# The square output matrices of S5, RG-LRU and RWKV as split three-term products

## The chip, the cores and the metric

One core of one Trainium2 chip runs the whole program. The metric is the device time of one execution in microseconds (us); the median of three runs is compared. The engines are TensorE (PE, with its weight loads shown as PEld), VectorE (DVE), ScalarE (ACT), GpSimd (POOL) and SyncE (SP), which here only issues the loads of weights.

## The reference, cut to what matters

A decoder trunk of two layers over 256 positions of width 1024, all in fp32. The part that the change touches is the hybrid mixing in the middle of each layer:

```python
    y_s5 = (y @ glu_w1) * jax.nn.sigmoid(y @ glu_w2)      # y: GELU of the S5 output, 512 channels
    ...
    y_lru = (h * jax.nn.gelu(zy)) @ lru_w_out             # h: RG-LRU scan
    ...
    y_rw = ((y + bonus) * g) @ rw_w_out                   # y: normalised RWKV-7 output
    ...
    merged = gates[:, :, 0] * y_s5 + gates[:, :, 1] * y_lru + gates[:, :, 2] * y_rw
    x = layer_norm(ALPHA * x + merged @ mix_w_out[l], ln2_g[l], ln2_b[l])
```

Around it stand a SwiGLU block before, cross-attention and a second SwiGLU block after. The four matrices glu_w1, glu_w2, lru_w_out and rw_w_out have 512 rows and 1024 columns; each layer has its own.

## The kernel before

Every weight matrix is cut into pieces of 128 x 1024 elements (512 KB). SP loads the pieces in one fixed order, `PIECES`, into a ring of 6 slots, `ring_raw`; a slot is loaded again when the piece in it has been multiplied (`s_piece`).

Most weights are multiplied as a split product. ACT copies a piece rounded to fp32r into `ring_hi`, a ring of only 3 slots (`hi_to`, through the helper at L1177; before the cast of split piece i it waits until split piece i - 3 has been multiplied). Then DVE (`lo_to`, L1564) or POOL (`piece_lo`, L2106) writes the remainder, raw minus hi, over the raw piece as `ring_lo`. `POOL_LO` lists the pieces whose remainder POOL takes, among them all of the branch gates; the rest is DVE's. The other operand is split the same way into a hi and a lo tensor. PE multiplies with `mm3` (L676, L677, L678): hi x hi, hi x lo, lo x hi, three fp32r matmuls into one bank.

The four square matrices are different: `PLAIN` names them (w1, w2, lru, rw), they are not cast and have no remainder, and `half_chunk` multiplies the raw piece by the unsplit fp32 operand (L689), 8 matmuls of 128 x 128 by 128 x 256 for each half chunk, which the profile records as 16. A chunk is 256 output columns in two halves m = 0 and 1 for the gates; a square chunk is 512 columns in two halves, 4 halves for each matrix. There are 32 such halves in the program.

Each engine runs a program written by hand, in order; `hi_to(kind, j, m)` means: cast all pieces up to this one, and with `further` also the next if it follows directly in `PIECES`. So where a cast stands in ACT's program decides when it can run, whatever the slots allow. In the middle of a layer the order is:

- ACT: the last GELUs of S5 (4 on `zu`), a wait for the RG-LRU result `ly` (`s_yl`), 8 sigmoids for RWKV's decay and in-context rate, gate evacuations, the exponentials of the RWKV decay, 4 scalings by r_k (`s_rks`), then the sigmoid of w2's product.
- DVE: 4 scans (L1826), each followed by a product (L1827), which give `ly`; then scans of the decay (L1834) and products L1836 to L1866, which build RWKV's operands, and in them the last reader of the first exponentials (L1859), for which ACT's third exponential waits.
- POOL: the remainders of gates 0 to 3, then nothing until it clears `W_bd` (L2177, L2178), which waits for the operands.
- PE: gates 0 to 3, the small RWKV products (L915 is the last of them and waits for 4 of ACT's sigmoids), w1 chunk 0, w2 chunk 0, the bonus sums (L926, which waits for `s_rks`), transposes (L932, L941) with the halves of w1 chunk 1 between, the products G (L956), w2 chunk 1, N (L965), gate 4.

Then comes the triangular solve: five rounds of small products and transposes (L977, L996, L1005), with a half chunk after each product; the fillers are gates 5, 6, 7 and lru 0, 1. The state recurrence over four chunks follows (L1021 to L1058) with gates 8 to 11 as fillers, and then the memory's k and v projections, rw chunks 0 and 1 between v 0 and v 1, and the output projection `mix`. `merge` on DVE (L1882, L1883, L1888, L1889) gathers the branches.

## Time and profile before

| | us |
|---|---|
| median of three runs | 1926.34 |
| lowest, highest | 1925.96, 1928.41 |
| profiled execution | 1927.2 |
| span in its trace | 1925.4 |
| PE busy | 1766.2 |
| DVE busy | 1251.6 |
| ACT busy | 778.7 |
| POOL busy | 601.9 |

The span runs from the first to the last instruction of the profiled execution. A matmul's recorded length contains its way through the array, so consecutive records overlap, and the cost of a block of matmuls is read from the start of its first record to the start of the next block. The two layers lie 948.5 us apart in the trace.

### The profile page before, as it was taken

The numbers are of one execution on the slowest core, as the hardware profiler recorded it, in microseconds if no ns is written. First come the engines' busy times: TensorE is split into PE (matmuls) and PEld (weight loads), VectorE is DVE, ScalarE is ACT, GpSimd is POOL, SyncE is SP. The second block draws the span as 40 slices with busy tenths as digits, with TensorE's granted clock in tenths as the row PEclk, the third lists the DMA queues.
The fourth block names the chain that finished last, engine by engine and source line by source line (L and its number), as shares of the span: only waits on it lengthen the run. The fifth ranks groups of instructions, "written<-read, shape, count | busy, mean of one in ns | idle before, by whom it ended". The sixth has DMA issues, their size and how long they took to land.

```text
span 1925.4 us, 29408 instructions
## 1 busy us (share of the span) xinstructions
PE 1766.2 (92%) x12308; PEld 1602.5 (83%) x12308; DVE 1251.6 (65%) x1430; ACT 778.7 (40%) x998; POOL 601.9 (31%) x370
## 2 busy tenths in 40 slices
PE   5999888888999999999999997988889899999997
PEld 5989866777988988899989896767789888879996
DVE  4587889985343675744476877999653365765445
ACT  3445512362224344544455444115521243544442
POOL 1141377522431030411151415774133400322112
PEclk9999988899899999999999999879998999999998
DMA  6655533332133554566666564223322345445663
GB/s 192 184 179 183 161 87 88 110 99 77 56 95 92 192 158 137 160 185 185 200 182 187 175 185 144 68 85 116 93 78 60 98 127 187 143 136 181 185 185 123
DMA packets 380603, 267.57 MB, mean 139 GB/s; under 512 B 21084, under 2 KB 361400, under 8 KB 380472
## 3 DMA queue, kind: packets, MB, share of 16 engines
q1 hardware_dynamic: 377624, 255.22, 44.5%
q10 hardware_dynamic: 2848, 10.49, 1.6%
q8 instruction: 97, 1.59, 0.3%
q14 instruction: 34, 0.28, 0.0%
HBM read 264.62 MB, written 1.05 MB: 138 GB/s over the span
## 4 chain that ended last, share of the span: by engine, by line
PE 64%; DVE 23%; issue 6%; ACT 3%; POOL 3%; DMA 1%; SPq 0%; DVEq 0%; POOLq 0%; ACTq 0%
PE bank L676 16%; PE bank L678 16%; PE bank L677 16%; DVE ring_lo L1564 5%; PE bank L689 5%; PE bank L996 2%; ACT ring_hi L1177 1%; PE bank L1005 1%; DVE work L1748 1%; DVE region_z L1944 1%; POOL work L2193 1%; DVE work L1752 1%; ACT work L1177 1%; DVE work L1785 1%; DVE small L1583 1%
## 5 line engine op out<-in xcount | busy, mean ns | idle before, releaser
L1564 DVE TENSOR_TENSOR ring_lo<-ring_raw,ring_hi 128x1024 fp32r<-128x1024 f32 x390 | 531.6, 1368 | 370.7 <-ACT ring_hi L1177 358.2
L1177 ACT ACTIVATE ring_hi<-ring_raw 128x1024 fp32r<-128x1024 f32 x444 | 468.0, 1057 | 587.8 <-PE bank L678 547.5
L676 PE MATMUL bank<-xT_hi,ring_hi 128*128 128x256 f32 x2224 | 650.7, 293 | 20.9 <-DVE ring_lo L1564 9.9
L677 PE MATMUL bank<-xT_lo,ring_hi 128*128 128x256 f32 x2224 | 641.1, 288 | 0.0
L678 PE MATMUL bank<-xT_hi,ring_lo 128*128 128x256 f32 x2224 | 640.3, 288 | 0.0
L676 PEld LDWEIGHTS bank<-xT_hi,ring_hi 128*128 128x128 f32 x2224 | 439.3, 198 | 37.9 <-issue 21.4
L677 PEld LDWEIGHTS bank<-xT_lo,ring_hi 128*128 128x128 f32 x2224 | 439.5, 198 | 1.8
L678 PEld LDWEIGHTS bank<-xT_hi,ring_lo 128*128 128x128 f32 x2224 | 438.8, 197 | 0.0
L2112 POOL TENSOR_TENSOR hT_lo<-work,hT_hi 128x512 fp32r<-128x512 f32 x44 | 79.4, 1807 | 508.5 <-ACT hT_hi L1177 508.0
L2106 POOL TENSOR_TENSOR ring_lo<-ring_raw,ring_hi 128x1024 fp32r<-128x1024 f32 x54 | 138.0, 2556 | 246.7 <-ACT ring_hi L1177 245.0
L678 PE MATMUL bank<-ring_hi,hT_lo 128*128 128x512 f32 x352 | 140.5, 399 | 0.0
L677 PE MATMUL bank<-ring_lo,hT_hi 128*128 128x512 f32 x352 | 140.2, 398 | 0.0
L676 PE MATMUL bank<-ring_hi,hT_hi 128*128 128x512 f32 x352 | 138.8, 394 | 0.9 <-POOL hT_lo L2112 0.5
L1177 ACT ACTIVATE work<-bank 128x512 f32<-128x512 f32 x94 | 53.9, 597 | 155.9 <-PE bank L678 69.4
L689 PE MATMUL bank<-region_z,ring_raw 128*128 128x256 f32 x384 | 87.2, 383 | 0.5 <-DVE region_a L1883 0.5
L689 PEld LDWEIGHTS bank<-region_z,ring_raw 128*128 128x128 f32 x384 | 72.7, 192 | 11.0 <-issue 0.9
L676 PEld LDWEIGHTS bank<-ring_hi,hT_hi 128*128 128x128 f32 x352 | 68.0, 193 | 15.7 <-issue 0.7
L2166 POOL TENSOR_TENSOR work<-work,region_r 128x512 f32<-128x512 f32 x32 | 66.3, 2072 | 46.9 <-DVE work L1752 46.9
L2080 POOL TENSOR_TENSOR small<-small,constants 128x1 f32<-128x1 f32 x16 | 10.9, 683 | 220.0 <-DVE small L1585 220.0
L678 PEld LDWEIGHTS bank<-ring_hi,hT_lo 128*128 128x128 f32 x352 | 66.7, 189 | 14.3
L677 PEld LDWEIGHTS bank<-ring_lo,hT_hi 128*128 128x128 f32 x352 | 66.8, 190 | 13.5
L1940 DVE TENSOR_TENSOR region_z<-bank,constants 128x512 f32<-128x512 f32 x20 | 13.8, 691 | 88.8 <-PE bank L1005 88.8
(277 smaller groups left out, 2729.1 us busy)
## 6 DMA issues: line engine op xcount, KB each, us to landing
...
```

What stands on the lines that cost most here:

```text
L676: mm(o, a[0], b[0], start=first, stop=False, **kw)
L677: mm(o, a[0], b[1], start=False, stop=False, **kw)
L678: return mm(o, a[1], b[0], start=False, stop=last, **kw)
L689: last = mm(o[:, c * T:(c + 1) * T], w[:, k, c * P:(c + 1) * P], src[:, k, :], start=(k == 0), stop=(k == NW - 1))
L996: last = mm(banks[4 + b][:, (q % 8) * C:(q % 8 + 1) * C], M_bd[:, q, :], Wst[:, q, :], start=True, stop=True)
L1005: last = mm(banks[6 + b][:, (q % 8) * C:(q % 8 + 1) * C], X_bd[:, q, :], Ysb[:, q, :], start=True, stop=True)
L1177: return nc.scalar.activation(o, i, func, **kw)
L1564: st.mark(tt(lo_flat(n), raw_flat(n), hi_flat(i), ALU.subtract), s_lo["dve"])
L1583: st.then(v.bn_stats(stats[t][:, 6 * h:6 * h + 6], x))
L2106: st.then(tt(lo_flat(n), raw_flat(n), hi_flat(i), ALU.subtract), s_lo["pool"])
L2112: st.mark(tt(lo, htmp[j % 2], hi, ALU.subtract), s_hl)
L2166: tt(s5n[:, 0, :, :], z, cs, ALU.mult)
```

## The change

The square pieces become split pieces like all the others. POOL takes the remainders of w1 and w2, DVE those of lru and rw. Three operands get a hi and a lo copy: `zu` (S5; hi by ACT, lo by POOL), `ly` (RG-LRU; hi by ACT, lo by POOL), and RWKV's gated result `wk[0]` as `yc` (hi by ACT, lo by DVE). PE uses `mm3` for them and waits for the lo copy where it waited for the operand. The hi copies lie in memory that is free then; `region_z` is shifted by a few elements for it. All casts and remainders are written into the programs of ACT, POOL and DVE:

```diff
-PLAIN = ("w1", "w2", "lru", "rw")
-POOL_LO = [("gate", j, m) for j in range(12) for m in range(2)] + [("g0", 0, 0), ("g1", 0, 0), ("z", 0, 0)]
+SQUARE = ("w1", "w2", "lru", "rw")
+POOL_LO = [(k, j, m) for k in ("w1", "w2") for j in range(2) for m in range(2)]
+POOL_LO += [("gate", j, m) for j in range(12) for m in range(2)] + [("g0", 0, 0), ("g1", 0, 0), ("z", 0, 0)]
...
-                if kind in PLAIN:
-                    n = number(kind, j, m)
-                    loaded(pe, n)
-                    w, o = slot(raw, n % RAW, NW, 256), claim(kind, j, m)
+                if kind in SQUARE:
+                    w, o = take(kind, j, m), claim(kind, j, m)
                     for c in range(2):
                         for k in range(NW):
-                            last = mm(o[:, c * T:(c + 1) * T], w[:, k, c * P:(c + 1) * P], src[:, k, :],
-                                      start=(k == 0), stop=(k == NW - 1))
+                            last = mm3(o[:, c * T:(c + 1) * T], [x[:, k, c * P:(c + 1) * P] for x in w],
+                                       [x[:, k, :] for x in src], k == 0, k == NW - 1)
...
-                pe.wait_ge(*at(s_ys5, NW))
-                by_channel("w1", 0, zu)
-                by_channel("w2", 0, zu)
+                pe.wait_ge(*at(s_zul, 1))
+                by_channel("w1", 0, zu_r)
+                by_channel("w2", 0, zu_r)
...
                     st.mark(f(zu[:, t, :], zu[:, t, :], ACT.Gelu_apprx_tanh), s_ys5)
-
+                act.wait_ge(*at(s_ys5, NW))
+                st.mark(f(zu_r[0], zu, ACT.Copy), s_zuh)
...
                 gate_evac(2)
+                hi_to("w1", 0, further=False)
...
                 gate_evac(3)
+                hi_to("w2", 0, 0, further=False)
...
+                hi_to("w2", 0, further=False)
                 glu_sigmoid(0)
+                hi_to("w1", 1, further=False)
...
+                hi_to("w2", 1, further=False)
                 hi_to("gate", 4, 0)
                 glu_sigmoid(1)
                 hi_to("gate", 5, 0)
                 gate_evac(4)
+                act.wait_ge(*at(s_yl, NW))
+                st.mark(f(ly_r[0], ly, ACT.Copy), s_lyh)
...
+                    if i == 2:
+                        hi_to("lru", 0, further=False)
+                    if i == 3:
+                        hi_to("lru", 1, further=False)
...
                 hi_to("v", 0)
+                act.wait_ge(*at(s_yrw, 1))
+                st.mark(f(yc_r[0], wk[0], ACT.Copy), s_ych)
                 v_evac(0)
+                hi_to("rw", 0, further=False)
...
+                    if i in (2, 3):
+                        lo_to("lru", i - 2, further=False)
...
+                lo_to("v", 0, further=False)
+                dve.wait_ge(*at(s_ych, 1))
+                st.mark(tt(yc_r[1], wk[0], yc_r[0], ALU.subtract), s_ycl)
                 lo_to("v", 1, 0)
...
+                pool.wait_ge(*at(s_zuh, 1))
+                st.mark(tt(zu_r[1], zu, zu_r[0], ALU.subtract), s_zul)
+                for k in ("w1", "w2"):
+                    piece_lo(k, 0, 0)
+                    piece_lo(k, 0, 1)
 
                 pool.wait_ge(*at(s_ops, 1))
                 st.then(g.memset(W_bd[0:C, :, C:P], 0.0))
                 st.then(g.memset(W_bd[C:P, :, 0:C], 0.0), s_p3)
+                for k in ("w1", "w2"):
+                    piece_lo(k, 1, 0)
+                    piece_lo(k, 1, 1)
                 gate_lo(4, 0)
                 gate_lo(4, 1)
+                pool.wait_ge(*at(s_lyh, 1))
+                st.mark(tt(ly_r[1], ly, ly_r[0], ALU.subtract), s_lyl)
```

In the rows below, a name in brackets is the semaphore that the instruction waits for: `rwkv_exponentials_used` is DVE's L1859, `rwkv_rk` DVE's L1843, `piece_multiplied` PE's progress through the pieces.

ACT before, from the evacuation of gate 2 to the scalings by r_k:

```order
L1177 ACTIVATE region_a<-bank 128x512 [waits piece_multiplied]
L1177 ACTIVATE work<-bank 128x512 [waits rwkv_lora_product]
L1177 ACTIVATE work<-bank 128x512
L1177 ACTIVATE region_a<-bank 128x512 [waits piece_multiplied]
L1177 ACT_TABLE_LOAD
L1177 ACTIVATE work<-work 128x1024 [waits rwkv_decay_sums]
L1177 ACTIVATE work<-work 128x1024
L1177 ACTIVATE work<-work 128x1024 [waits rwkv_exponentials_used]
L1177 ACTIVATE work<-work,param_columns 128x256 [waits rwkv_lora_product,rwkv_rk]
L1177 ACTIVATE work<-work,param_columns 128x256 x3
```

ACT now, from just behind the same evacuation:

```order
L1181 ACTIVATE ring_hi<-ring_raw 128x1024 [waits weights_loaded5,piece_multiplied]
L1181 ACTIVATE work<-bank 128x512 [waits rwkv_lora_product]
L1181 ACTIVATE work<-bank 128x512
L1181 ACTIVATE region_a<-bank 128x512 [waits piece_multiplied]
L1181 ACTIVATE ring_hi<-ring_raw 128x1024 [waits weights_loaded0,piece_multiplied]
L1181 ACT_TABLE_LOAD
L1181 ACTIVATE work<-work 128x1024 [waits rwkv_decay_sums]
L1181 ACTIVATE work<-work 128x1024
L1181 ACTIVATE work<-work 128x1024 [waits rwkv_exponentials_used]
L1181 ACTIVATE work<-work,param_columns 128x256 [waits rwkv_lora_product,rwkv_rk]
L1181 ACTIVATE work<-work,param_columns 128x256 x3
L1181 ACTIVATE ring_hi<-ring_raw 128x1024 [waits weights_loaded1,piece_multiplied]
```

Three casts have come in: w1 (0, 1) behind gate 2's evacuation, w2 (0, 0) behind gate 3's, and w2 (0, 1) behind the scalings by r_k. (L1177 has become L1181.)

POOL before, from the remainders of gates 0 to 3 to those of gate 4:

```order
L2106 TENSOR_TENSOR ring_lo<-ring_raw,ring_hi 128x1024 [waits weights_hi,s5_rotated_back]
L2106 TENSOR_TENSOR ring_lo<-ring_raw,ring_hi 128x1024 [waits weights_hi,weights_lo_pool] x7
L2177 MEMSET work 64x16x64 [waits rwkv_operands,weights_lo_pool]
L2178 MEMSET work 64x16x64 [waits pool_chain]
L2106 TENSOR_TENSOR ring_lo<-ring_raw,ring_hi 128x1024 [waits weights_hi,prep_pool]
L2106 TENSOR_TENSOR ring_lo<-ring_raw,ring_hi 128x1024 [waits weights_hi,weights_lo_pool]
```

POOL now:

```order
L2130 TENSOR_TENSOR ring_lo<-ring_raw,ring_hi 128x1024 [waits weights_hi,s5_rotated_back]
L2130 TENSOR_TENSOR ring_lo<-ring_raw,ring_hi 128x1024 [waits weights_hi,weights_lo_pool] x7
L2200 TENSOR_TENSOR zu_lo<-region_z,zu_hi 128x1024 [waits s5_gelu_hi,weights_lo_pool]
L2130 TENSOR_TENSOR ring_lo<-ring_raw,ring_hi 128x1024 [waits weights_hi]
L2130 TENSOR_TENSOR ring_lo<-ring_raw,ring_hi 128x1024 [waits weights_hi,weights_lo_pool] x3
L2206 MEMSET work 64x16x64 [waits rwkv_operands,weights_lo_pool]
L2207 MEMSET work 64x16x64 [waits pool_chain]
L2130 TENSOR_TENSOR ring_lo<-ring_raw,ring_hi 128x1024 [waits weights_hi,prep_pool]
L2130 TENSOR_TENSOR ring_lo<-ring_raw,ring_hi 128x1024 [waits weights_hi,weights_lo_pool] x5
```

zu_lo and four remainders (w1 and w2, chunk 0) now stand ahead of the two MEMSETs, and four more (w1 and w2, chunk 1) ahead of gate 4's two.

DVE before, from the last two products of RWKV's result to the first merges of rw:

```order
L1987 TENSOR_TENSOR work<-work 128x1024
L1988 TENSOR_TENSOR work<-work 128x1024 [waits dve_chain]
L1564 TENSOR_TENSOR ring_lo<-ring_raw,ring_hi 128x1024 [waits weights_hi,rwkv_gated]
L1564 TENSOR_TENSOR ring_lo<-ring_raw,ring_hi 128x1024 [waits weights_hi] x3
L1888 TENSOR_TENSOR region_a<-region_a,bank 128x512 [waits piece_multiplied,gates_activated]
L1889 TENSOR_TENSOR region_a<-region_a 128x512 [waits dve_chain]
L1888 TENSOR_TENSOR region_a<-region_a,bank 128x512 [waits piece_multiplied,gates_activated,merged_banks_read]
L1889 TENSOR_TENSOR region_a<-region_a 128x512 [waits dve_chain]
```

DVE now, the same place:

```order
L2008 TENSOR_TENSOR work<-work 128x1024
L2009 TENSOR_TENSOR work<-work 128x1024 [waits dve_chain]
L1583 TENSOR_TENSOR ring_lo<-ring_raw,ring_hi 128x1024 [waits weights_hi,rwkv_gated]
L1583 TENSOR_TENSOR ring_lo<-ring_raw,ring_hi 128x1024 [waits weights_hi]
L2018 TENSOR_TENSOR yc_lo<-work,yc_hi 128x1024 [waits rwkv_gated_hi]
L1583 TENSOR_TENSOR ring_lo<-ring_raw,ring_hi 128x1024 [waits weights_hi] x6
L1907 TENSOR_TENSOR region_a<-region_a,bank 128x512 [waits piece_multiplied,gates_activated]
L1908 TENSOR_TENSOR region_a<-region_a 128x512 [waits dve_chain]
L1907 TENSOR_TENSOR region_a<-region_a,bank 128x512 [waits piece_multiplied,gates_activated,merged_banks_read]
L1908 TENSOR_TENSOR region_a<-region_a 128x512 [waits dve_chain]
```

yc_lo and four remainders of rw stand between the remainders of v 0 and the first merge, and the remainders of v 1 behind them, still ahead of the merge.

## Rows read from the trace of the kernel before

**Rows 1.** The page: busy time by engine, and shares of the chain that ended last

```profile
PE 1766.2 (92%) x12308; PEld 1602.5 (83%) x12308; DVE 1251.6 (65%) x1430; ACT 778.7 (40%) x998; POOL 601.9 (31%) x370
...
PE 64%; DVE 23%; issue 6%; ACT 3%; POOL 3%; DMA 1%; SPq 0%; DVEq 0%; POOLq 0%; ACTq 0%
```

**Rows 2.** The page, groups: count | busy us, mean ns | idle before <- releaser

```profile
L2106 POOL TENSOR_TENSOR ring_lo<-ring_raw,ring_hi 128x1024 fp32r<-128x1024 f32 x54 | 138.0, 2556 | 246.7 <-ACT ring_hi L1177 245.0
```

**Rows 3.** Timeline, TensorE: start us, us, engine, line, operation, count [idle <- releaser]

```profile
415.20 3.78 PE L915 MATMUL bank<-work,up_weights 128*128 128x256 f32 x8 [6.45 <-ACT work L1177]
418.77 14.31 PE L689 MATMUL bank<-region_z,ring_raw 128*128 128x256 f32 x64
```

**Rows 4.** Timeline, TensorE, layer 0, around the RWKV output matrix

```profile
640.71 0.36 PE L676 MATMUL bank<-ring_hi,memT_hi 128*128 128x256 f32 x1 [0.61 <-DVE ring_lo L1564]
...
646.54 13.98 PE L689 MATMUL bank<-work,ring_raw 128*128 128x256 f32 x64
660.17 0.47 PE L676 MATMUL bank<-ring_hi,memT_hi 128*128 128x256 f32 x1
...
666.11 0.39 PE L676 MATMUL bank<-ring_hi,merged_hi 128*128 128x512 f32 x1
...
668.89 0.40 PE L676 MATMUL bank<-ring_hi,merged_hi 128*128 128x512 f32 x1
```

**Rows 5.** Timeline, VectorE, 363 to 374 us

```profile
362.90 1.52 DVE L1785 SCALAR_TENSOR_TENSOR work<-region_z,param_columns,work 128x256 f32<-128x256 f32 x3
...
365.60 2.49 DVE L1783 TENSOR_SCALAR work<-region_z,param_columns 128x256 f32<-128x256 f32 x1
368.12 5.68 DVE L1785 SCALAR_TENSOR_TENSOR work<-region_z,param_columns,work 128x256 f32<-128x256 f32 x3
```

**Rows 6.** Timeline, GpSimd, 363 to 374 us

```profile
364.59 5.81 POOL L2106 TENSOR_TENSOR ring_lo<-ring_raw,ring_hi 128x1024 fp32r<-128x1024 f32 x2 [8.94 <-ACT ring_hi L1177]
370.60 2.40 POOL L2106 TENSOR_TENSOR ring_lo<-ring_raw,ring_hi 128x1024 fp32r<-128x1024 f32 x1 [0.20 <-ACT ring_hi L1177]
```

**Rows 7.** Timeline, VectorE, RG-LRU end and RWKV operands, layer 0

```profile
413.12 0.43 DVE L1827 TENSOR_TENSOR region_z<-work,region_z 128x256 f32<-128x256 f32 x1
...
419.12 1.38 DVE L1840 TENSOR_SCALAR work<-work,param_columns,small 128x256 f32<-128x256 f32 x4 [0.18 <-PE bank L915]
...
427.00 1.42 DVE L1859 TENSOR_TENSOR work<-work 128x256 f32<-128x256 f32 x4
```

**Rows 8.** Timeline, ScalarE, the same stretch

```profile
408.69 1.33 ACT L1177 ACTIVATE region_z<-region_z 128x256 f32<-128x256 f32 x4
...
413.58 3.02 ACT L1177 ACTIVATE work<-bank,param_columns 128x256 f32<-128x256 f32 x8 [2.25 <-DVE region_z L1827]
...
419.99 0.60 ACT L1177 ACTIVATE region_a<-bank 128x512 f32<-128x512 f32 x1
...
429.42 1.69 ACT L1177 ACTIVATE work<-work,param_columns 128x256 f32<-128x256 f32 x4
```

**Rows 9.** Timeline, GpSimd, the same stretch

```profile
402.70 2.50 POOL L2106 TENSOR_TENSOR ring_lo<-ring_raw,ring_hi 128x1024 fp32r<-128x1024 f32 x1 [4.22 <-ACT ring_hi L1177]
431.26 0.94 POOL L2177 MEMSET work<- 64x1024 f32 x1 [26.05 <-DVE small L1866]
```

**Rows 10.** Timeline, TensorE, start of the triangular solve

```profile
472.72 2.41 PE L977 MATMUL bank<-constants,work 128*128 128x128 f32 x16 [2.70 <-DVE work L1930]
```

**Rows 11.** Timeline, VectorE, start of the triangular solve

```profile
470.13 1.17 DVE L1925 COPY work<-region_z 64x512 f32<-64x512 f32 x2 [0.87 <-PE bank L977]
```

**Rows 12.** Windows: us, busy PE, PEld, DVE, ACT, POOL, granted clock, DMA share, GB/s

```profile
474.00:484.00 10.00, 10.00 (x50) 10.00 (x48) 1.29 (x2) 3.05 (x5) 2.56 (x2) 0.50 0.01 2
...
1423.00:1433.00 10.00, 10.00 (x89) 9.89 (x88) 2.43 (x4) 3.84 (x6) 2.69 (x2) 1.00 0.16 54
```

**Rows 13.** Timeline, ScalarE, RWKV output matrix

```profile
653.55 1.06 ACT L1177 ACTIVATE ring_hi<-ring_raw 128x1024 fp32r<-128x1024 f32 x1 [4.42 <-DMA ring_raw<-in_xa_wkv_dram]
```

**Rows 14.** Timeline, VectorE, RWKV output matrix

```profile
655.78 0.68 DVE L1888 TENSOR_TENSOR region_a<-region_a,bank 128x512 f32<-128x512 f32 x1
```

More of the change, by code:

```diff
@@ L148 @@
 for _n, _x in enumerate(PIECES * L):
-    if _x[0] not in PLAIN:
-        _who = "pool" if _x in POOL_LO else "dve"
-        SPLIT_AT[_n] = len(SPLIT_AT)
-        LO_AT[_n] = (_who, sum(w == _who for w, _ in LO_AT.values()))
+    _who = "pool" if _x in POOL_LO else "dve"
+    SPLIT_AT[_n] = len(SPLIT_AT)
+    LO_AT[_n] = (_who, sum(w == _who for w, _ in LO_AT.values()))
 SPLITS = list(SPLIT_AT)
@@ L256, in trunk @@
         V_AT = 1024 + 8 * (T + 1)
-        LX_AT = 1024 + RWT * (T + 1)
+        LX_AT = 1024 + RWT * (T + 1) + 2
         lx = view(reg_z, LX_AT, NW, T + 3)
-        ly = view(reg_z, LX_AT + NW * (T + 3), NW, T)
+        ly = view(reg_z, LX_AT + NW * (T + 3) + 4, NW, T)
         memtok = view(reg_z, LX_AT, 2, D)
+        zu_r = [rounded("zu_hi", z_at, LX_AT, NW, T), rounded("zu_lo", z_at, 0, NW, T)]
+        ly_r = [rounded("ly_hi", z_at, LX_AT, NW, T), rounded("ly_lo", z_at, LX_AT + NW * (T + 3) + 4, NW, T)]
+        yc_r = [rounded("yc_hi", w_at, 9216, NW, T), rounded("yc_lo", w_at, 4096, NW, T)]
         b_raw = [view(reg_z, 256 * i, NS, 16) for i in range(2)]
@@ L398, in trunk @@
         s_ys5 = sem("s5_gelu", 4)
+        s_zuh, s_zul = sem("s5_gelu_hi", 1), sem("s5_gelu_lo", 1)
+        s_lyh, s_lyl = sem("lru_y_hi", 1), sem("lru_y_lo", 1)
+        s_ych, s_ycl = sem("rwkv_gated_hi", 1), sem("rwkv_gated_lo", 1)
         s_conv = sem("lru_conv", 4)
@@ L943, in _ @@
                 last.then_inc(s_tok, 1)
-                half_chunk("w1", 1, 1, zu)
+                half_chunk("w1", 1, 1, zu_r)
                 for g in range(4):
@@ L958, in _ @@
                     last.then_inc(s_G, 1)
[L959 removed]
+                by_channel("w2", 1, zu_r)
                 pe.wait_ge(*at(s_Ge, 8))
@@ L983, in _ @@
                 turn_pairs(W_bd)
-                fill = [("gate", 5, xT), ("gate", 6, xT), ("gate", 7, xT), ("lru", 0, ly), ("lru", 1, ly)]
+                fill = [("gate", 5, xT), ("gate", 6, xT), ("gate", 7, xT), ("lru", 0, ly_r), ("lru", 1, ly_r)]
                 pe.wait_ge(*at(s_Ta, 2))
@@ L1095, in _ @@
                 memory_values(0)
-                pe.wait_ge(*at(s_yrw, 1))
-                by_channel("rw", 0, wk[0])
-                by_channel("rw", 1, wk[0])
+                pe.wait_ge(*at(s_ycl, 1))
+                by_channel("rw", 0, yc_r)
+                by_channel("rw", 1, yc_r)
                 memory_values(1)
@@ L1413, in _ @@
                         gate_evac(5 + i)
+                    if i == 2:
+                        hi_to("lru", 0, further=False)
+                    if i == 3:
+                        hi_to("lru", 1, further=False)
                     if i == 4:
-                        hi_to("gate", 8)
+                        hi_to("gate", 8, further=False)
                     turned(X_bd, i + 3)
```

10 lines of the change are left out of this document (5 added, 5 removed).

## The prediction

> **What bounds the kernel now.** The page comes first: PE is busy 92% of the span and carries 64% of the chain that ended last, DVE 23%, POOL 3% [rows 1]. A saving on PE therefore counts where PE's own queue is the last to finish, and not where PE waits for DVE or ACT. The second view is PE's timeline around the square matrices. In the S5 stage PE is idle for 6.45 us until ACT's sigmoids release L915, and then runs all four halves of w1 and w2, chunk 0, in one block from 418.77 to 433.0 [rows 3]. The third view, DVE and ACT over the same stretch, shows what runs beside that block: the RG-LRU scans end at 413.55, ACT's sigmoids run from 413.58, DVE builds RWKV's operands with no gap over 0.2 us from 417.7 to 428.4 (L1859), and ACT's scalings by r_k end at 431.1 [rows 7, 8]. PE's next product, the bonus sums, needs exactly those scalings. So here two chains end within 2 us of each other: PE's block at 433.0, and scans, sigmoids, DVE products, exponential, scalings at 431.1. POOL does nothing in all that time: its last remainder ends at 405.2, and the next operation starts at 431.26 after 26.05 us of idle time [rows 9]. Layer 1 shows the same times 948.5 us later, so each cost below counts twice.
>
> **What is removed: PE time.** The four plain halves of rw take 660.17 - 646.54 = 13.63 us, 3.41 each; the two split halves of v 0 before them (48 matmuls) take 646.54 - 640.71 = 5.83 us, 2.92 for 24 matmuls, which is what a square half becomes [rows 4]. That is 0.49 us for each of 32 halves, 16 us in all if all of it counted.
>
> The Trainium skill's page "FP8 and Floating Point Precision" (Matmul Precision) says that true fp32 takes four passes through the array; three passes would then take 2.56 instead of 3.41 us, 27 us in all. The rows show 2.92, so the measurement decides against the page's ratio.
>
> **What is added, S5 stage.** ACT gets 32 casts of 1.06 us [rows 13] and 6 hi copies of that size; POOL gets 16 remainders and 4 lo copies of 2.56 us [rows 2]; DVE gets 16 remainders and 2 lo copies. Most lie beside other work. What counts is where they stand in the three programs.
>
> First, POOL against DVE. From 362.90 three L1785 on DVE take 1.52 us. From 368.12 the same three take 5.68 us, while POOL subtracts two remainders (the second of the pair from 364.59, and the one at 370.60); L1783 before them took 2.49 us for one [rows 5, 6]. So a DVE operation with SBUF operands that is issued while a POOL remainder runs ends just after it, and one remainder costs a busy DVE about 2.1 us. Now four POOL operations come into the stretch where DVE is on the chain:
> - zu_lo and the remainder of w1 (0, 0). ACT's GELUs end at 410.02 [rows 8], zu_hi at 411.1, so POOL starts zu_lo at 411.2 and the remainder right behind. DVE has two scans and two products of `ly` left. Each POOL operation holds up one of them by 2.0: `ly` is ready at 417.5 instead of 413.55, +4.0. The eight sigmoids and L915 move with it (L915 has the low clock before and after).
> - The remainders of w1 (0, 1) and w2 (0, 0). Their casts stand behind the evacuations of gate 2 and gate 3 (the latter ends at 420.6 before, 424.6 now [rows 8]). Both remainders fall between L1836 and L1844, where DVE has no gap: +2.3 each.
>
> L1859 thus ends at 428.4 + 8.6 = 437.0, the third exponential follows, and the scalings end at 439.7 instead of 431.1. Second, ACT's order: the cast of w2 (0, 1) stands behind these scalings. It ends at 440.8, POOL's remainder at 443.3. PE has finished w2 (0, 0) near 432 and waits for 11 us. The last half then runs from 443.3 and needs about 4.6 us rather than 2.9, because after such a gap the granted clock is at its low level (after the 6.45 us gap L915's stretch is slow too [rows 3]; the windows show 0.50, which is 1.2 of 2.4 GHz, and 1.00 [rows 12]). The bonus sums start near 447.9, before at 432.9: **+15.0**.
>
> After them, w1 (1, 0) is cast only behind the sigmoid of w2's product, and its remainder ends about 2.4 us after PE could start: +2.4. The remainders behind it keep up (2.56 on POOL against 2.92 on PE). The four halves of chunk 1 save 4 x 0.5 = 2.0. Sum of the S5 stage: +15.4.
>
> **Solve.** ly_hi (ACT) and ly_lo (POOL) come ahead of POOL's first copy of the solve. ly_lo runs from about 469.4 to 471.8 (in the clock of before), so DVE's two copies at 470.13 are held up, and with them the transposes that waited 2.70 us until 472.72 [rows 10, 11]: +1.9. The halves of lru are fillers in rounds 3 and 4, with PE last to finish there: -4 x 0.5 = -2.0. One cast stands ahead of a copy on ACT that releases round 3: +1.0. Sum: +0.9.
>
> **RWKV output.** ACT casts rw (0, 0) and yc_hi by 642.9, DVE has yc_lo and the remainder by 645.4, before PE arrives at 646.54: nothing. rw (0, 1) waits 0.3. rw then ends at 658.5, 1.7 early. But the cast of v (1, 1) needs its place in the ring of three, free when rw (1, 0) is multiplied at 655.6; it ran at 653.55 before [rows 13]. Its remainder stands ahead of DVE's first merge, which moves from 655.78 [rows 14] to 658.1. The remainder of the second piece of mix stands behind all four merges and ends near 669.8; PE reached that piece at 668.89, 2.78 after the first [rows 4], and would now be there at 667.1. So the gain is lost and +0.9 comes out.
>
> **Sum.** 15.4 + 0.9 + 0.9 = 17.2 us a layer, 34 in all. The profiled execution took 1927.2 us with a span of 1925.4; 1.8 us lie around the span, and the median is 1926.3. The median after is 1926.3 + 34 = **1960**.
>
> The unknown prices: how often DVE is held up (0 to 2.3 us for each of the four operations and twice: down to -17, and up to +5, if a remainder meets two operations); the clock in the solve. The same first round, with the same work, has 0.50 in layer 0 and 1.00 in layer 1 [rows 12], and a longer wait at its start (4.6 instead of 2.7 us) can bring the low clock to layer 1 (+4) while another round loses it (-4). I take 0 and keep -8 to +8.
>
> **Rivals.**
> 1. *The port costs nothing* (DVE's operations slip in ahead of POOL's). ACT's order alone remains: scalings end at 431.1, cast 432.2, remainder 434.7, last half until 438 or, at the low clock, 439.4: +5 to +6.5 instead of +15; with the rest 8 us a layer, about 1942. For it: many of DVE's operations are short, 0.42 us. The Trainium skill's page "SBUF — State Buffer" (Who interferes with whom) says that whichever of the two issues second blocks fully; with DVE first, POOL alone would pay. Rows 5 and 6 show DVE paying when it is busy without a gap. Against: a queued POOL operation is issued as soon as the one before ends.
> 2. *PE's saving decides* (faster). The casts are early enough and the chain of DVE has slack that I don't see: PE saves 16 us less two small waits: 1912. For it: PE's 92%. Against: the cast of w2 (0, 1) can't be issued before the scalings at 431.1, and PE would want that piece at about 427.
> 3. *Worse still.* The long waits drop the clock in the solve of both layers and more operations meet: 1975 to 1985. It decides if the low clock covers two rounds more in each layer, at 4 us each.
> 4. *No difference*: the port's cost is small and the late piece is paid back by PE's saving in rw and lru: 1923 to 1930.
>
> **How the numbers follow.** My forecast, the two chains lengthened by port and order, 1945 to 1974: 0.63. Rival 1: 0.14. Rival 2: 0.09. Rival 3: 0.10. Rival 4: 0.04. The range takes the forecast, rival 1 and the lower part of rival 3: 1937 to 1976. A difference of 0.2% (3.9 us) is about what can be told from none in this kernel. Faster by more: 0.10; within: 0.04; slower by more: 0.86.
>
> **What would show it.** In the trace after: L1827's last product near 417.5 with one or two of the four L1826 and L1827 taking about 2.4 us; L1840 to L1844 with two operations lengthened by 2.3; POOL's fifth remainder of the stage ending near 443 and PE idle before w2 (0, 1) by about 11 us, released by POOL; a wait of about 2.4 us before w1 (1, 0); DVE's two copies at the start of the solve (L1925, now L1944) taking 1.7 us more; mix starting near 664 (shifted by what came before) and waiting some 2.7 us before its second piece. The forecast is wrong if PE's idle time before w2 (0, 1) is under 3 us, or if DVE's operations between 411 and 428 keep their lengths.

## The result, and the profile of the changed kernel

| | before | changed kernel |
|---|---|---|
| median, us | 1926.99 (4 runs, 1925.96 to 1928.41) | 1961.19 (4 runs, 1957.93 to 1962.48) |
| span of the profiled execution, us | 1925.4 | 1958.3 |
| mean granted TensorE clock | 0.955 | 0.945 |

The ratio is 1.0174, with a 95% interval from 1.0157 to 1.0192: the change costs 34.2 us. The forecast was 1960.

The page of the changed kernel, busy time, chain and one group (count | busy us, mean ns | idle time before, releaser):

```profile
PE 1751.0 (89%) x12564; PEld 1600.2 (82%) x12564; DVE 1292.0 (66%) x1448; ACT 815.0 (42%) x1036; POOL 651.9 (33%) x390
...
PE 59%; DVE 26%; issue 6%; ACT 4%; POOL 4%; DMA 1%; SPq 0%; DVEq 0%; POOLq 0%; ACTq 0%
...
L682 PE MATMUL bank<-zu_hi,ring_hi 128*128 128x256 f32 x128 | 39.5, 308 | 26.7 <-POOL ring_lo L2130 26.7
```

PE is busy 15.2 us less than in [rows 1], close to the 16 us of the forecast, and the program is 34 us longer. In the chain PE lost 5 points, and DVE, ACT and POOL gained 3, 1 and 1. The last line is a new wait: 26.7 us of PE's idle time stand before the products of S5, released by GpSimd's remainders. Where these are, TensorE's timeline of layer 0 shows (start us, us, engine, line, operation, count, [idle before, releaser]; L919 answers to L915, L930 to L926, L969 to L965, L981 to L977):

```profile
420.86 3.66 PE L919 MATMUL bank<-work,up_weights 128*128 128x256 f32 x8 [10.43 <-ACT work L1181]
424.08 0.56 PE L682 MATMUL bank<-zu_hi,ring_hi 128*128 128x256 f32 x1
...
444.20 0.58 PE L682 MATMUL bank<-zu_hi,ring_hi 128*128 128x256 f32 x1 [11.12 <-POOL ring_lo L2130]
...
448.92 1.88 PE L930 MATMUL bank<-work,constants 128*128 128x512 f32 x4
...
456.75 0.39 PE L682 MATMUL bank<-zu_hi,ring_hi 128*128 128x256 f32 x1 [2.47 <-POOL ring_lo L2130]
...
475.16 2.08 PE L969 MATMUL bank<-region_a,work 64*64 64x64 f32 x64
...
489.96 3.65 PE L981 MATMUL bank<-constants,work 128*128 128x128 f32 x16 [4.07 <-DVE work L1949]
```

In [rows 3] the wait before L915 was 6.45 us, here it is 10.43. Three halves follow from 424.08 to 433.1, 3.0 us each; then PE stands for 11.12 us, and the fourth half takes from 444.20 to 448.92, 4.72 us. ScalarE and GpSimd show who kept it waiting:

```profile
439.03 1.69 ACT L1181 ACTIVATE work<-work,param_columns 128x256 f32<-128x256 f32 x4
440.62 1.04 ACT L1181 ACTIVATE ring_hi<-ring_raw 128x1024 fp32r<-128x1024 f32 x1
```

```profile
412.94 2.78 POOL L2200 TENSOR_TENSOR zu_lo<-region_z,zu_hi 128x1024 fp32r<-128x1024 f32 x1 [6.06 <-ACT zu_hi L1181]
415.68 2.52 POOL L2130 TENSOR_TENSOR ring_lo<-ring_raw,ring_hi 128x1024 fp32r<-128x1024 f32 x1
423.84 3.03 POOL L2130 TENSOR_TENSOR ring_lo<-ring_raw,ring_hi 128x1024 fp32r<-128x1024 f32 x1 [5.64 <-ACT ring_hi L1181]
427.22 2.41 POOL L2130 TENSOR_TENSOR ring_lo<-ring_raw,ring_hi 128x1024 fp32r<-128x1024 f32 x1 [0.36 <-ACT ring_hi L1181]
441.81 2.34 POOL L2130 TENSOR_TENSOR ring_lo<-ring_raw,ring_hi 128x1024 fp32r<-128x1024 f32 x1 [12.17 <-ACT ring_hi L1181]
```

The scalings by r_k end at 440.7 (before 431.1, [rows 8]), the cast of w2 (0, 1) follows, and its remainder ends at 444.15. The first four GpSimd operations lie where VectorE is busy without a gap. Its timeline there (L1845 and L1846 are the scan and product of `ly`, L1859 is L1840 of before, L1878 is L1859 of before):

```profile
413.62 2.38 DVE L1846 TENSOR_TENSOR region_z<-work,region_z 128x256 f32<-128x256 f32 x1
416.04 2.71 DVE L1845 TENSOR_TENSOR_SCAN work<-region_a,work 128x256 f32<-128x256 f32 x1
418.78 0.43 DVE L1846 TENSOR_TENSOR region_z<-work,region_z 128x256 f32<-128x256 f32 x1
...
424.66 5.44 DVE L1859 TENSOR_SCALAR work<-work,param_columns,small 128x256 f32<-128x256 f32 x4
...
436.62 1.42 DVE L1878 TENSOR_TENSOR work<-work 128x256 f32<-128x256 f32 x4
```

One product takes 2.38 instead of 0.43 us [rows 7], one scan 2.71 instead of 0.69 (the length of its sisters), and the four L1859 take 5.44 instead of 1.38 [rows 7], since two remainders meet them. That is four GpSimd operations and 1.95 + 2.02 + 4.06 = 8.0 us.

All runs below are compared over the same stretches, each from the start of one record of TensorE to the start of another. Stage: first small RWKV product (L905 of before) to the bonus sums L926. Chunk 1: L926 to L965. Gate 4: L965 to the first L996. Solve: the first L996 to the first L1021. Rest: L1021 to the transposes of the LayerNorm behind `mix` (L784).

| us, layer 0 / layer 1 | stage | chunk 1 | gate 4 | solve | rest |
|---|---|---|---|---|---|
| before | 33.1 / 33.2 | 26.4 / 26.4 | 15.6 / 15.3 | 89.3 / 86.6 | 132.0 / 131.9 |
| changed kernel | 47.4 / 47.8 | 26.2 / 26.2 | 18.2 / 18.1 | 88.0 / 83.7 | 132.5 / 132.5 |
| only w1, w2 split | 47.2 / 47.5 | 27.8 / 26.2 | 15.3 / 16.1 | 88.2 / 88.8 | 131.9 / 131.9 |
| only lru split | 32.7 / 33.1 | 26.4 / 26.4 | 18.0 / 18.2 | 83.7 / 83.7 | 131.9 / 131.9 |
| only rw split | 32.7 / 33.1 | 26.4 / 26.4 | 16.0 / 15.6 | 88.9 / 89.3 | 132.5 / 132.5 |
| idle subtractions | 39.1 / 39.1 | 28.5 / 28.5 | 16.7 / 16.6 | 85.0 / 88.5 | 133.4 / 131.9 |
| early cast | 41.6 / 41.5 | 28.1 / 28.1 | 18.2 / 18.1 | 88.1 / 83.7 | 132.5 / 132.5 |
| remainders on VectorE | 37.1 / 37.5 | 26.2 / 26.3 | 18.2 / 17.9 | 88.0 / 85.2 | 134.0 / 132.6 |
| partly split | 33.1 / 33.2 | 24.0 / 24.0 | 16.6 / 16.5 | 84.9 / 86.7 | 131.0 / 129.5 |
| before, late remainders | 32.7 / 33.2 | 26.4 / 26.4 | 16.0 / 15.3 | 78.7 / 77.9 | 135.0 / 133.2 |
| partly split, late remainders | 32.7 / 32.7 | 24.0 / 24.0 | 16.8 / 16.8 | 75.4 / 75.4 | 132.1 / 132.2 |

Of the changed kernel's cost, 28.9 us are in the two stages. All five stretches of both layers together are 30.8 us longer; the spans of the two traces differ by 32.9 us, and 1.7 of the other 2.1 lie ahead of the first changed instruction.

### The profile page after: what moved, and what is told of

Same layout as the page of the kernel before. It is cut to its first block, busy times and chain, and to the rows that moved or that the text cites. A ratio compares the mean times of both kernels' runs of the same rounds, so it can differ in the third digit from the quotient of the medians.

```text
span 1958.3 us, 30046 instructions
## 1 busy us (share of the span) xinstructions
PE 1751.0 (89%) x12564; PEld 1600.2 (82%) x12564; DVE 1292.0 (66%) x1448; ACT 815.0 (42%) x1036; POOL 651.9 (33%) x390
## 4 chain that ended last, share of the span: by engine, by line
PE 59%; DVE 26%; issue 6%; ACT 4%; POOL 4%; DMA 1%; SPq 0%; DVEq 0%; POOLq 0%; ACTq 0%
PE bank L682 17%; PE bank L683 16%; PE bank L684 16%; DVE ring_lo L1583 6%; PE bank L1000 2%; ACT ring_hi L1181 2%; DVE work L1767 1%; PE bank L1009 1%; ACT work L1181 1%; DVE work L1771 1%; DVE region_z L1963 1%; POOL work L2228 1%; DVE work L1765 1%; DVE work L1764 1%; DVE work L1804 1%
## 5 line engine op out<-in xcount | busy, mean ns | idle before, releaser
L1583 DVE TENSOR_TENSOR ring_lo<-ring_raw,ring_hi 128x1024 fp32r<-128x1024 f32 x406 | 550.8, 1362 | 358.8 <-ACT ring_hi L1181 345.5
L1181 ACT ACTIVATE ring_hi<-ring_raw 128x1024 fp32r<-128x1024 f32 x476 | 501.2, 1057 | 604.0 <-PE bank L684 575.2
L2130 POOL TENSOR_TENSOR ring_lo<-ring_raw,ring_hi 128x1024 fp32r<-128x1024 f32 x70 | 178.0, 2542 | 286.9 <-ACT ring_hi L1181 285.1
L1181 ACT ACTIVATE work<-bank 128x512 f32<-128x512 f32 x94 | 53.9, 597 | 121.9 <-PE bank L684 72.9
L2190 POOL TENSOR_TENSOR work<-work,region_r 128x512 f32<-128x512 f32 x32 | 66.3, 2073 | 47.4 <-DVE work L1771 47.4
L684 PEld LDWEIGHTS bank<-ring_hi,hT_lo 128*128 128x128 f32 x352 | 66.9, 190 | 14.3
L1181 ACT ACTIVATE region_z<-bank 128x512 f32<-128x512 f32 (+1 forms) x62 | 33.5, 540 | 94.4 <-PE bank L684 44.7
L682 PE MATMUL bank<-zu_hi,ring_hi 128*128 128x256 f32 x128 | 39.5, 308 | 26.7 <-POOL ring_lo L2130 26.7
```

Of the source, the lines that this page charges most:

```text
L682: mm(o, a[0], b[0], start=first, stop=False, **kw)
L684: return mm(o, a[1], b[0], start=False, stop=last, **kw)
L1181: return nc.scalar.activation(o, i, func, **kw)
L1583: st.mark(tt(lo_flat(n), raw_flat(n), hi_flat(i), ALU.subtract), s_lo["dve"])
L2130: st.then(tt(lo_flat(n), raw_flat(n), hi_flat(i), ALU.subtract), s_lo["pool"])
L2190: tt(s5n[:, 0, :, :], z, cs, ALU.mult)
```

## The experiments

**1. Each matrix alone.** Three kernels keep one part of the change each and leave the other square matrices unsplit, with their copies, casts and remainders gone. The edit, for w1 and w2 alone:

```diff
+PLAIN = [('lru', 0), ('lru', 1), ('rw', 0), ('rw', 1)]
...
-                pe.wait_ge(*at(s_lyl, 1))
+                pe.wait_ge(*at(s_yl, NW))
...
-                by_channel("rw", 0, yc_r)
+                by_channel("rw", 0, wk[0])
```

> The kernel of the change with w1 and w2 split and lru and rw left as unsplit fp32, with nothing else of theirs added. Theory (the S5 stage holds nearly all of the loss): the trace of the changed kernel shows the start of its gate 4 shifted by +14.2 us in layer 0 and +14.4 in layer 1; without ly's copies the solve keeps its length, so 2 x 14.3 = 28.6 us: 1955.5 us, 1951 to 1959. Rival A (the loss is partly one of the solve, where longer waits bring the low clock): under 1948. Rival B (TensorE's saving of 0.49 us for each of 16 halves decides): 1919.

> The kernel of the change with lru split and w1, w2 and rw left unsplit. Theory: ly_lo on GpSimd ahead of its copy in the solve costs more (+2.6 us a layer up to the first Y product in the changed kernel) than the four shorter halves give back (2.0), and with the cast in front of a copy the sum is +1.3 a layer: 1929 us, 1926 to 1932. Rival (TensorE is last to finish in those rounds and the copies are covered): -2.0 a layer, 1922.5.

> The kernel of the change with rw split and the other three left unsplit. Theory: rw ends 1.7 us earlier, and the remainders of v (1, 1) and of mix's second piece on VectorE give it all back: +0.6 to +0.9 a layer, 1928 us, 1926 to 1930. Rival (the saving arrives): -2.0 a layer, 1922.5. If these three kernels add up, their differences from the kernel before sum to about 34 us.

The kernel before took 1927.68 us beside these. Only w1 and w2: 1957.37 (ratio 1.0150, 1.0133 to 1.0167), as the theory said, and the table shows why: the stage is as long as in the full change. Only rw: 1928.36 (1.0005, 0.9996 to 1.0014), the 0.5 us a layer of the last column. Only lru: 1923.38 (0.9977, 0.9967 to 0.9986). There my number, 1929, missed, and the rival's, 1922.5, came out, though not for its reason: it had the copies covered, and the cost at the start of the solve is there (gate 4 takes 2.4 and 2.9 us more). ly_lo on GpSimd and the copy of VectorE that it holds up (1.17 us in [rows 11]), in this kernel:

```profile
468.03 2.35 POOL L2223 TENSOR_TENSOR ly_lo<-region_z,ly_hi 128x1024 fp32r<-128x1024 f32 x1 [18.20 <-ACT ly_hi L1192]
```

```profile
468.87 2.54 DVE L1955 COPY work<-region_z 64x512 f32<-64x512 f32 x2 [0.87 <-PE bank L992]
```

But behind it the solve is 5.6 us shorter in layer 0 and 2.9 in layer 1. Windows over the solve of layer 1, for before and for this kernel (us, busy PE, PEld, DVE, ACT, POOL, granted clock, DMA share, GB/s):

```profile
1423.30:1509.94 86.64, 81.32 (x610) 78.55 (x609) 34.31 (x38) 20.37 (x31) 37.22 (x18) 0.94 0.22 66
```

```profile
1421.35:1505.05 83.70, 77.28 (x642) 76.27 (x641) 39.02 (x42) 23.92 (x34) 34.96 (x18) 0.96 0.23 70
```

The clock is a part of it. The kernel before has 89.3 us in layer 0 at a granted clock of 0.909 and 86.6 in layer 1 at 0.941, for the same work: 2.7 us go with 0.032 of clock. By that rate, an estimate, the 0.018 between the two rows above (0.941 and 0.959 with a third digit) are 1.6 of the 2.9 us, and 1.3 are the shorter halves, net of the cast; the prediction had 1.0. In layer 0 the clock is 0.959 against 0.909, 4.3 of the 5.6 us by the same rate, and 1.3 remain. My 1929 took the sum of layer 0 of the changed kernel (+1.3), whose solve has the clock of 0.91.

By the medians the three parts sum to 29.7 - 4.3 + 0.7 = 26 us, while the whole costs 34. In the traced executions the parts do add: over the five stretches of the table they are +31.1, -3.8 and +3.6, together 30.9 us, and the whole is +30.8. So the 8 us between the medians are in none of these stretches. The mean granted clocks differ too (0.953, 0.956 and 0.956 for the parts, 0.945 for the whole, 0.955 for before), but part of that lies ahead of the first changed instruction, and where the 8 us come from stays open.

**2. GpSimd's reading alone.** The kernel before with four more subtractions a layer:

```diff
+                pool.wait_ge(*at(s_ys5, NW))
+                st.then(tt(idle_out, xT[0][:, 0:4, :], xT[1][:, 0:4, :], ALU.subtract))
+                st.then(tt(idle_out, xT[0][:, 0:4, :], xT[1][:, 0:4, :], ALU.subtract))
+                pool.wait_ge(*at(s_gact, 3))
+                st.then(tt(idle_out, xT[0][:, 0:4, :], xT[1][:, 0:4, :], ALU.subtract))
+                pool.wait_ge(*at(s_gact, 4))
+                st.then(tt(idle_out, xT[0][:, 0:4, :], xT[1][:, 0:4, :], ALU.subtract))
                 pool.wait_ge(*at(s_ops, 1))
```

> The kernel before, with all four matrices unsplit, and four more GpSimd subtractions of 128 x 1024 elements a layer whose result nothing reads: two back to back when ACT's last GELU of S5 is done, one after the evacuation of gate 2, one after that of gate 3. No cast, no order and no wait of the other engines is changed. Theory (a GpSimd subtraction holds up VectorE where that has no gap, 2.0 us each): the scalings by r_k end 8 us later (439 instead of 431.1), and the bonus sums start at about 439.3 instead of 432.9: +6.4 a layer, 1939 us, 1936 to 1943, with two of the last six scans and products of ly at 2.4 us or more. Rival (the port costs nothing, only ACT's order does): 1926 to 1928, and VectorE's operations keep their lengths.

> As the kernel with four idle GpSimd subtractions a layer, but each subtraction replaced by two MEMSETs of 128 x 1024 elements, which read nothing; same waits, same places. Theory (VectorE is held up by the subtraction's reading of two operands, not by the waits put into GpSimd's program or by its writes): 1926 to 1929 us, and the scans and products of ly keep 0.69 and 0.43 us. Rival (any GpSimd work, or the semaphores, hold VectorE up): about 1940, as with the subtractions.

With the subtractions 1941.68 us (ratio 1.0077, 1.0062 to 1.0092), with the MEMSETs 1928.86 beside 1928.86 of before (0.9999, 0.9990 to 1.0008). VectorE's timeline with the subtractions:

```profile
412.15 2.38 DVE L1827 TENSOR_TENSOR region_z<-work,region_z 128x256 f32<-128x256 f32 x1
414.56 2.71 DVE L1826 TENSOR_TENSOR_SCAN work<-region_a,work 128x256 f32<-128x256 f32 x1
...
423.10 3.19 DVE L1836 TENSOR_TENSOR work<-work 128x1024 f32<-128x1024 f32 x1
426.32 3.31 DVE L1840 TENSOR_SCALAR work<-work,param_columns,small 128x256 f32<-128x256 f32 x4
```

As in the changed kernel one product and one scan of `ly` are held up, by the same amounts, and the other two subtractions cost 1.97 (3.19 against 1.22) and 1.93 (3.31 against 1.38). With the MEMSETs beside the last scans of `ly`:

```profile
413.01 0.69 DVE L1826 TENSOR_TENSOR_SCAN work<-region_a,work 128x256 f32<-128x256 f32 x1
413.73 0.43 DVE L1827 TENSOR_TENSOR region_z<-work,region_z 128x256 f32<-128x256 f32 x1
```

```profile
412.95 0.95 POOL L2179 MEMSET region_z<- 128x1024 f32 x1
413.96 0.95 POOL L2180 MEMSET region_z<- 128x1024 f32 x1
```

So it is neither GpSimd's writing nor the waits in its program. What is left is the subtraction with its two operands; that the reading of them does it, and not the arithmetic, no run here separates. The stage is 6.0 us longer with the subtractions alone, of 14.4 in the changed kernel. Another 2.1 come in chunk 1, which this kernel computes as before. TensorE waits 2.35 us for the scalings, and the transposes L932 behind the bonus sums take 3.29 us instead of 1.94. The windows over chunk 1 of layer 0, before and here, have granted clocks of 1.00 and 0.88. This I had not put into the 1939.

```profile
432.92:459.29 26.37, 24.05 (x165) 19.80 (x163) 11.60 (x18) 6.54 (x9) 5.00 (x3) 1.00 0.29 80
```

```profile
440.38:468.88 28.50, 26.42 (x164) 21.38 (x164) 11.61 (x18) 6.54 (x9) 6.60 (x4) 0.88 0.23 64
```

TensorE's rows of this kernel:

```profile
440.38 3.13 PE L926 MATMUL bank<-work,constants 128*128 128x512 f32 x4 [2.35 <-ACT work L1177]
445.06 3.29 PE L932 MATMUL bank<-constants,region_a 128*128 128x128 f32 x16 [1.54 <-DVE work L1870]
```

The Trainium skill's page "SBUF — State Buffer" (Who interferes with whom) says that a VectorE instruction with two SBUF inputs contends with a GpSimd instruction that reads SBUF, and not with one that only writes it. These two runs agree, with 2.0 us a subtraction and nothing for a MEMSET. It also says that a VectorE instruction with at most one SBUF input does not contend outside its two-port modes. The changed kernel's masks of G have a PSUM and an SBUF operand. Eight of them take 5.04 us with three GpSimd remainders beside them all the time, and 5.04 us too in the kernel before, where GpSimd is done after half of them. L1840 and the copies of L1925 read one tensor and were held up all the same (1.38 to 3.31 us, 1.17 to 2.54); whether they ran in such a mode no trace shows. The masks, and GpSimd beside them:

```profile
465.63 5.04 DVE L1923 TENSOR_TENSOR region_r<-bank,constants 128x512 f32<-128x512 f32 x8 [2.65 <-PE bank L960]
```

```profile
463.98 7.28 POOL L2130 TENSOR_TENSOR ring_lo<-ring_raw,ring_hi 128x1024 fp32r<-128x1024 f32 x3 [4.49 <-ACT ring_hi L1181]
```

**3. ACT's order.** The changed kernel with one cast moved:

```diff
                 gate_evac(3)
-                hi_to("w2", 0, 0, further=False)
+                hi_to("w2", 0, further=False)
...
-                hi_to("w2", 0, further=False)
                 glu_sigmoid(0)
```

> The kernel of the change with one cast moved: that of w2 (0, 1) stands ahead of ACT's exponentials instead of behind the scalings by r_k. Theory (port and ACT's order add up): its remainder now runs near 430 and holds VectorE up once more, so the scalings end at 442.7 (440.7 in the changed kernel), but PE no longer waits 11 us for the piece: the bonus sums start at about 442.9 instead of 448.9, -6.0 us a layer: 1949 us, 1946 to 1953. Rival (only ACT's order counts, and TensorE's block sets the end): bonus sums at 436, -12.9 a layer, 1935.

It took 1947.09 us (ratio to before 1.0097, 1.0082 to 1.0112), against 1.0174 for the change: -15 us by the ratios, -10 by the two spans (1958.3 and 1948.3, the latter from the slowest of four executions), expected -12. TensorE and GpSimd:

```profile
440.57 3.75 PE L930 MATMUL bank<-work,constants 128*128 128x512 f32 x4 [7.35 <-ACT work L1181]
445.87 3.24 PE L936 MATMUL bank<-constants,region_a 128*128 128x128 f32 x16 [1.54 <-DVE work L1888]
```

```profile
426.94 2.40 POOL L2129 TENSOR_TENSOR ring_lo<-ring_raw,ring_hi 128x1024 fp32r<-128x1024 f32 x1
```

PE now waits 7.35 us, and for the scalings, no longer for the piece. The stage is 41.6 and 41.5 us, 5.8 and 6.3 less: that is the share of ACT's order, net of one more remainder beside VectorE. A part of it is lost again in chunk 1, 28.1 us instead of 26.2: behind the wait, at a mean granted clock of 0.86 there instead of 1.00, the bonus sums L930 take 3.75 us instead of 1.88 and the transposes L936 3.24 instead of 1.94. The rival's 1935 is out.

**4. The same remainders on VectorE.** As the kernel before this one, with zu_lo and the four remainders of chunk 0 in VectorE's program:

```diff
+                dve.wait_ge(*at(s_zuh, 1))
+                st.mark(tt(zu_r[1], zu, zu_r[0], ALU.subtract), s_zul)
+                lo_to("w1", 0, 0, further=False)
                 r_, k_, v_ = (zrw[:, a:a + 4, 1:T + 1] for a in (0, 4, 8))
...
                 st.then(tt(sw, dec, sw, ALU.subtract), s_dec)
+                lo_to("w1", 0, further=False)
...
                 st.then(tt(k_, k_, rk, ALU.mult))
+                lo_to("w2", 0, 0, further=False)
...
                 st.then(ins, s_ex)
+                lo_to("w2", 0, further=False)
```

> The kernel of the change with the cast of w2 (0, 1) ahead of the exponentials, and with zu_lo and the four remainders of chunk 0 taken from GpSimd and given to VectorE: zu_lo and w1 (0, 0) behind the last product of ly, w1 (0, 1) behind the decay's products, w2 (0, 0) behind the product of k, w2 (0, 1) behind the last reader of the first exponentials. Theory (a remainder of 1.23 us on VectorE itself is cheaper than one of 2.5 us beside it on GpSimd): two fall into VectorE's 1.7 us of idle time (+0.8), two cost 1.2 each, the last one lies in the idle time before the third exponential; the scalings end near 434.5, the last half of w2 runs until 435.8, and from the first small RWKV product to the bonus sums it takes 36 us instead of 41.5: 1936 us, 1931 to 1940. Rival (the work counts, wherever it is done): no gain over 1947.

It took 1939.45 us (1.0053, 1.0035 to 1.0071), 8 us better than the early cast alone. VectorE's own remainders, and what PE waits for:

```profile
415.25 1.22 DVE L1849 TENSOR_TENSOR zu_lo<-region_z,zu_hi 128x1024 fp32r<-128x1024 f32 x1
416.39 1.22 DVE L1582 TENSOR_TENSOR ring_lo<-ring_raw,ring_hi 128x1024 fp32r<-128x1024 f32 x1
...
421.25 1.23 DVE L1582 TENSOR_TENSOR ring_lo<-ring_raw,ring_hi 128x1024 fp32r<-128x1024 f32 x1
```

```profile
434.15 0.39 PE L682 MATMUL bank<-zu_hi,ring_hi 128*128 128x256 f32 x1 [4.69 <-DVE ring_lo L1582]
```

The stage is 37.1 and 37.5 us, where 36 was expected; the last half takes 4.5 us behind a wait of 4.69, as the fourth half did in the changed kernel. A subtraction that VectorE does itself costs it 1.23 us, one that GpSimd does beside it costs it 2.0: given to GpSimd, the work made a full VectorE later than when VectorE did it itself. The split of chunk 0 still loses: VectorE's chain has no room for it.

**5. Split only where nothing pays.** w1 and w2 stay unsplit in chunk 0. The rest is split and put into gaps. The core of the edit against the changed kernel:

```diff
+PLAIN = [('w1', 0), ('w2', 0)]
...
-                hi_to("w2", 0, further=False)
+                hi_to("w1", 1)
                 glu_sigmoid(0)
...
+                lo_to("w1", 1, 0, further=False)
+                done_chunk(dve, "w2", 0)
+                dve.wait_ge(*at(s_zuh, 1))
+                st.mark(tt(zu_r[1], zu, zu_r[0], ALU.subtract), s_zul)
                 dve.wait_ge(*at(s_bon, 1))
...
                 turned(X_bd, 2)
+                dve.wait_ge(*at(s_lyh, 1))
+                st.mark(tt(ly_r[1], ly, ly_r[0], ALU.subtract), s_lyl)
...
+                hi_to("rw", 0, further=False)
                 v_evac(0)
-                hi_to("rw", 0, further=False)
+                hi_to("rw", 1, 0, further=False)
```

> A version that keeps the split only where nothing on the chain pays for it: w1 and w2 chunk 0 unsplit; chunk 1 split, its casts by ACT right behind the scalings, zu_lo and all four remainders by VectorE in its gaps, none by GpSimd; lru split, with ly_hi and ly_lo behind the copies at the start of the solve (ly_lo on VectorE) and each cast behind the copies that release a round; rw split, with the casts of rw, v and mix one by one in the order in which ring_hi comes free and the first merges ahead of v's remainders. Theory (TensorE's 0.49 us a half arrives wherever neither VectorE's nor ACT's chain is touched): 12 halves a layer, -5.9 us: 1915 us, 1911 to 1920. Rival (other waits take the gain): 1923 or more.

It took 1914.87 us (ratio 0.9929, 0.9914 to 0.9944): the theory's 1915. The stage is unchanged, chunk 1 is 2.4 us shorter in each layer, and the rest 1.0 and 2.4. Gate 4 takes 1.0 and 1.2 us more, which the theory did not have. The solve is 4.4 us shorter in layer 0 (clock 0.94 instead of 0.91) and shows no gain in layer 1 (86.7), at the lower clock that it had in layer 0 before. So the total fits, but the solve gave 4.4 and 0.0 us where the theory had 2.0 in each layer.

**6. The same price in the kernel before.** GpSimd's remainders in the solve start beside VectorE's addition that closes a round (L1944). A wait in GpSimd's program puts them behind it:

```diff
                     if i < 3:
+                        if i:
+                            pool.wait_ge(*at(s_Wst, i + 1))
                         gate_lo(5 + i, 0)
                         gate_lo(5 + i, 1)
+                pool.wait_ge(*at(s_Wst, 6))
                 gate_lo(8, 1)
```

> The kernel before, all four matrices unsplit, with one wait added to GpSimd: in the solve its two remainders of gates 6, 7 and 8 (1) start behind VectorE's addition that closes the round, not beside it. That addition takes 3.42 us instead of 1.23 in those rounds, and TensorE waits 1.50 us for it. Theory (the port is dear wherever VectorE is on the chain, in the kernel before too): -1.5 us in each of two rounds and up to -2.2 at the end of the solve, 3.0 to 5.2 a layer: 1918 us, 1915 to 1921. Rival (the remainders then hold up the copies that follow, or come too late for the gates' halves): 1926 or more.

> The partly split version with GpSimd's remainders in the solve moved: those of gates 6 and 7 start behind VectorE's addition that closes the round, that of gate 8 (0) goes to VectorE, that of gate 8 (1) stands ahead of GpSimd's part of the last round, and the next one waits for the merges of lru. Theory (the two gains add up; in the solve the wait on the held up addition also brought the low clock): the rounds of the solve take 76 us a layer instead of 84.9 and 86.7: 1897 us, 1892 to 1903. Rival (the halves of lru are no longer last to finish once the wait is gone, or the low clock comes back elsewhere): 1904 to 1912.

The first took 1914.94 us (0.9934, 0.9918 to 0.9951), from a later start of some GpSimd remainders and with all four matrices unsplit. That is just outside the expected 1915 to 1921: the gain was put at 3.0 to 5.2 us a layer. The view of L1944, in the kernel before and in this one (durations in ns, smallest, median, largest):

```profile
L1944 DVE TENSOR_TENSOR region_z<-region_z x10: 1224/3414/3422, 492.1 to 1505.1; 128x1024 f32<-128x1024 f32 x10
...
  PE bank L996: 6.0, 4
```

```profile
L1944 DVE TENSOR_TENSOR region_z<-region_z x10: 1224/1226/1227, 487.8 to 1488.7; 128x1024 f32<-128x1024 f32 x10
```

Six of the ten additions took 3.4 us and PE waited four times 1.5 us for them; now all take 1.23, and nobody waits. The solve is 10.7 and 8.7 us shorter, much more than the 3.0 us a layer of those waits. Windows over the solve of both layers, before and here:

```profile
474.93:564.26 89.33, 84.03 (x610) 81.25 (x609) 34.30 (x38) 20.03 (x30) 36.86 (x18) 0.91 0.21 64
```

```profile
474.14:552.82 78.68, 77.14 (x609) 74.61 (x609) 27.72 (x38) 20.04 (x30) 32.61 (x18) 0.99 0.23 69
1414.93:1492.87 77.94, 76.40 (x609) 73.87 (x609) 27.73 (x38) 20.39 (x31) 33.38 (x18) 1.00 0.23 69
```

The granted clock rises from 0.91 and 0.94 to 0.99 and 1.00. Of the 10.7 us in layer 0, 3.8 are less idle time of TensorE (89.33 - 84.03 before, 78.68 - 77.14 here) and 6.9 are shorter busy time for the same matmuls. The clock can account for these, by an estimate from the same rows: 9% of 89.33 us is 8.0 us lost before, 1% of 78.68 is 0.8 here. Where the low clock lies in the kernel before is seen behind its two waits of 1.50 us in layer 0, which end at 495.61 and at 515.11:

```profile
500.00:505.00 5.00, 5.00 (x25) 5.00 (x25) 0.00 (x0) 1.54 (x2) 0.00 (x0) 0.52 0.00 0
515.00:520.00 5.00, 4.89 (x43) 4.90 (x44) 1.34 (x3) 1.19 (x2) 2.27 (x1) 1.00 0.02 4
```

Behind the first, TensorE runs at its low level of 1.2 GHz (0.5); behind the second, an equal wait, it stays at the high one. So such a wait can bring the low clock and need not. A part comes back in the rest (+3.1 and +1.3): the last remainders now meet the merges of lru.

The second kernel joins both ideas and mends that: 1899.32 us (0.9853, 0.9839 to 0.9868), the best here, 28 us faster than the kernel before, with a mean granted clock of 0.960. The solve takes 75.4 us in both layers. The two gains, 14.0 and 13.9 us, add up.

## Why the prediction was right

The size and the sign were right, and the place: the S5 stage. That the total came within 2 us is in part luck. The prediction had 34.4 us in the two layers; in the traces the stretches of the table have 30.8, and the rest of the measured 34.2 lies outside them. The start of L905, ahead of every change, varies from 398.9 to 401.6 us between the traces of this case.

- **PE's saving**: 16 us, measured 15.2 in PE's busy time. The halves of S5 take 2.9 to 3.0 us at the high clock.
- **The port, first pair**: +4.0, measured 3.97 at L919 over what layer 0 brought with it (+1.7 at L905, ahead of the first changed instruction; +1.4 there in the kernel with idle subtractions).
- **The port, second pair**: +2.3 each, measured 2.0 each. I had it on any of L1836 to L1844; both met L1840's four.
- **ACT's order**: PE idle for "11 us", measured 11.12; the last half "about 4.6", measured 4.72. The bonus sums +15.0, measured 14.3 and 14.6. The difference is the 0.6 us of the second pair.
- **Chunk 1**: +2.4 - 2.0, measured a wait of 2.47 and -0.1 over the stretch.
- **Solve**: here one term was mis-sized. ly_lo was put at +1.9 and cost 2.6 and 2.9: the copies 1.4 (the wait before the second transposes went from 2.70 [rows 10] to 4.07), and the transposes behind the longer wait another 1.2 (3.65 us against 2.41). The halves and the cast were put at -1.0; with the clock of layer 0 (0.91 before and after) they gave -1.3. The sum of both is +1.3 in layer 0 and -0.1 in layer 1, predicted +0.9. Layer 1 has its sum from the clock, 0.96 instead of 0.94 in the solve: some 1.6 us by the rate of experiment 1. The prediction had left the clock at 0 with -8 to +8 for both layers.
- **RWKV output**: +0.9, measured +0.6 in both layers. The way there was not quite mine. I had one wait of 2.7 us before the second piece of mix. TensorE's timeline has two, and the first, before v (1, 0), is for a bank that a late merge frees:

```profile
676.48 0.39 PE L682 MATMUL bank<-ring_hi,memT_hi 128*128 128x256 f32 x1 [0.89 <-DVE region_a L1908]
...
686.51 0.51 PE L682 MATMUL bank<-ring_hi,merged_hi 128*128 128x512 f32 x1 [1.24 <-DVE ring_lo L1583]
```

Rival 1 (the port costs nothing) is refuted by the idle subtractions, 14 us by themselves. Rival 2's saving exists, but only in a kernel that keeps the split off chunk 0: the partly split one. Rival 3's clock did not fall further in the solve of the changed kernel (0.91 and 0.96 against 0.91 and 0.94); it fell in the stage, from 0.90 to 0.78 and 0.75, and in gate 4, from 0.97 and 1.00 to 0.88 and 0.91:

```profile
493.40:581.42 88.02, 81.59 (x641) 80.58 (x641) 39.03 (x42) 23.92 (x34) 34.95 (x18) 0.91 0.22 67
1458.64:1542.36 83.72, 77.29 (x643) 76.28 (x641) 39.04 (x42) 23.92 (x34) 35.07 (x18) 0.96 0.24 71
```

What I did not see in the profile of before: the same price was already being paid there. [rows 5] and [rows 6] gave me the number, and L1944's 3.42 us stood in the solve with PE waiting for it; I used the rows only to cost the change.
